# Splitting the token dimension of the first FFN's up-projection: two products of 256 tokens with the same weights in the place of one of 512

## The reference

```python
def swiglu_ffn(x, wi, wo):
    g, u = jnp.split(x @ wi, 2, axis=-1)      # wi: 1024 x 5632
    return (jax.nn.silu(g) * u) @ wo          # wo: 2816 x 1024

for i in range(DEPTH):                        # DEPTH = 2
    x = x + 0.5 * swiglu_ffn(rmsnorm(x, ffn1_norm[i]), ffn1_wi[i], ffn1_wo[i])
    ...                                       # mLSTM and window attention, merged
    x = x + 0.5 * swiglu_ffn(rmsnorm(x, ffn2_norm[i]), ffn2_wi[i], ffn2_wo[i])
    ...
```

## Time and profile before

| | |
|---|---|
| runs | 3436.26, 3437.9, 3438.53 us; median 3437.9 |
| the profiled execution | 3438.94 us, span 3437.2 us |
| PE busy | 3404.9 us (99%), 15506 products |
| PEld busy | 2747.4 us (80%), 15506 loads |
| DVE, ACT, POOL busy | 1599.5, 1040.8, 1546.8 us |
| mean granted clock of TensorE | 0.997 of 2.4 GHz |

### The profile page before, as it was taken

The page is one execution under the profiler, slowest core; times in us unless marked ns, Lnnn a source line. Parts: engine busy times, 40 slices in busy tenths (PEclk is TensorE's granted clock), DMA queues, the critical chain, the costliest instruction groups (busy, mean ns, idle before and its releaser), DMA issues.

```text
span 3437.2 us, 43454 instructions
## 1 busy us (share of the span) xinstructions
PE 3404.9 (99%) x15506; PEld 2747.4 (80%) x15506; DVE 1599.5 (47%) x1957; ACT 1040.8 (30%) x1383; POOL 1546.8 (45%) x1160
## 2 busy tenths in 40 slices
PE   8999999999999999999999999999999999999998
PEld 7888876788888888887678888877788887778887
DVE  5442235754423544223665442377480726647161
ACT  3222234332222322223433222246421123632112
POOL 4444432354444444443335444443354443335452
PEclk9999999999999999999999999999999999999999
DMA  4332322233333333342223333332233323223332
GB/s 149 98 97 94 110 74 68 74 98 98 98 103 93 93 96 98 98 111 74 62 74 104 98 93 103 95 93 48 68 98 98 98 92 81 51 65 108 94 98 80
DMA packets 496157, 311.25 MB, mean 91 GB/s; under 512 B 41792, under 2 KB 454827, under 8 KB 496043
## 3 DMA queue, kind: packets, MB, share of 16 engines
q1 hardware_dynamic: 494316, 307.21, 30.4%
q10 hardware_dynamic: 1727, 2.45, 0.2%
HBM read 305.94 MB, written 3.67 MB: 90 GB/s over the span
## 4 chain that ended last, share of the span: by engine, by line
issue 54%; POOL 35%; PE 10%; POOLq 1%; DVE 0%; DMA 0%; ACT 0%; ACTq 0%; DVEq 0%
POOL wl L488 35%; PE bank L507 2%; PE bank L511 2%; PE bank L512 2%; PE bank L530 1%; PE bank L526 1%; PE bank L532 1%; POOLq L485 0%; POOLq L483 0%; PE bank L533 0%; DMA onehot<-in_onehot_dram 0%; DVE x_sb L1748 0%; DVE acc L2340 0%; ACT out_tok L1668 0%; POOLq L488 0%
## 5 line engine op out<-in xcount | busy, mean ns | idle before, releaser
L488 POOL TENSOR_TENSOR wl<-raw,wh 128x512 fp32r<-128x512 f32 x1152 | 1545.7, 1364 | 1853.3 <-ACT wh L1288 1853.1
L1288 ACT ACTIVATE wh<-raw 128x1024 fp32r<-128x1024 f32 x576 | 608.2, 1057 | 1578.7 <-PE bank L507 747.0
L526 PE MATMUL bank<-xh,wh 128*128 128x512 f32 x2384 | 933.4, 392 | 0.0
L530 PE MATMUL bank<-xl,wh 128*128 128x512 f32 x2384 | 928.4, 389 | 0.0
L532 PE MATMUL bank<-xh,wl 128*128 128x512 f32 x2086 | 812.6, 390 | 0.0
L526 PEld LDWEIGHTS bank<-xh,wh 128*128 128x128 f32 x2384 | 448.0, 188 | 105.0 <-issue 12.3
L530 PEld LDWEIGHTS bank<-xl,wh 128*128 128x128 f32 x2384 | 448.2, 188 | 91.9
L507 PE MATMUL bank<-hh,wh 128*128 128x512 f32 (+1 forms) x1216 | 473.2, 389 | 0.0
L512 PE MATMUL bank<-hh,wl 128*128 128x512 f32 (+1 forms) x1216 | 473.0, 389 | 0.0
L511 PE MATMUL bank<-hl,wh 128*128 128x512 f32 (+1 forms) x1216 | 473.0, 389 | 0.0
L532 PEld LDWEIGHTS bank<-xh,wl 128*128 128x128 f32 x2086 | 392.0, 188 | 81.9
(11 more groups left out here) (390 smaller groups left out, 3112.9 us busy)
## 6 DMA issues: line engine op xcount, KB each, us to landing
raw<-in_ffn_wi_dram SPq DMA_DIRECT2D x176, 512.0 KB, 3.7
raw<-in_mlp_w_dram SPq DMA_DIRECT2D x128, 512.0 KB, 3.8
raw<-in_w_in_dram SPq DMA_DIRECT2D x102, 512.0 KB, 3.6
raw<-in_ffn_wo_dram SPq DMA_DIRECT2D x88, 512.0 KB, 3.6
raw<-in_w_out_dram SPq DMA_DIRECT2D x32, 512.0 KB, 3.8
raw<-in_w_ple_gate_dram SPq DMA_DIRECT2D x16, 512.0 KB, 3.8
raw<-in_w_a_dram SPq DMA_DIRECT2D x8, 512.0 KB, 3.4
raw<-in_w_b_dram SPq DMA_DIRECT2D x8, 512.0 KB, 3.3
```

What stands on the lines that cost most here:

```text
L488: last = gp.tensor_tensor(wl[j][:, part], raw[j % RAW_SLOTS][:, part], wh[j][:, part].bitcast(F32), ALU.subtract)
L526: first = pe.matmul(out[0:width, :], h[:, c:c + width], rh[:, k, :], start=k == 0, stop=False)
L530: pe.matmul(out[0:width, :], h[:, c:c + width], rl[:, k, :], start=False, stop=False)
L1288: act.activation(wh[n % SPLIT_SLOTS][:], raw[n % RAW_SLOTS][:], ACT.Copy).then_inc(s.hi_ready, 1)
```

## The change

In the ten-pass loop of each layer's first FFN (k = 0), each product of 512 tokens becomes two products of 256 tokens, first the left half of the bank and then the right half, with the same stationary tile. The order of the three kinds of product and of the eight feature tiles stays. The signal `slab_used` leaves with the unit's first half product, `tile_ready` with the last one. The second FFN's loop (k = 2), `first_units`, the down-projections and all other engines' programs stay as they are.

```diff
+            def unit_by_halves(B, L, n, t, rh, rl, i, step):
+
+                take_slab(B, L, n, i, step)
+                out = open_tile(B, L, t, i, step)
+                h, l = wh[n % SPLIT_SLOTS], wl[n % SPLIT_SLOTS]
+                for kt in range(KT):
+                    w = slice(kt * P, (kt + 1) * P)
+                    for a, b in ((h, rh), (h, rl), (l, rh)):
+                        for half in range(2):
+                            tok = slice(half * 2 * P, (half + 1) * 2 * P)
+                            last = pe.matmul(out[:, tok], a[:, w], b[:, kt, tok], start=kt == 0 and a is h and b is rh and half == 0,
+                                             stop=kt == KT - 1 and a is l and half == 1)
+                            if kt == 0 and a is h and b is rh and half == 0:
+                                last.then_inc(s.slab_used, 1)
+                last.then_inc(s.tile_ready, 1)
...
                 with pe.Fori(1, FT // 2) as i:
                     for u in range(4):
-                        unit(Block1, L, n + u, t + u, xh, xl, i, 4)
+                        if k == 0:
+                            unit_by_halves(Block1, L, n + u, t + u, xh, xl, i, 4)
+                        else:
+                            unit(Block1, L, n + u, t + u, xh, xl, i, 4)
```

## The result

The kernel after the change takes 3463.6 us (median of 6 runs, 3462.1 to 3464.3) where the one before takes 3438.9 us (6 runs, 3436.3 to 3442.0): a ratio of 1.0072, with a 95% interval of 1.0059 to 1.0084, some 24.7 us more. The prediction was 3440.5 us in a range of 3435 to 3466. The range holds the time, but only because it reached up to a rival's price; the forecast's own range (3435 to 3445) doesn't hold it, and "slower by over 0.2%", which had a chance of 0.37, came true. The profiled execution took 3464.2 us, its span 3462.4 us.

A forecast was written before the change was run, and what follows sets the result against it. TensorE, busy 3404.9 of 3437.2 us, was taken to bound the kernel. 3840 half products at 0.7 ns more each added 2.6 us to 3438.9, nothing for issue or clock: 3441.5, or 3440.5 for the median; range 3435 to 3466.

The forecast's parts named there:

- slower by over 0.2%: Whole kernel more than 6.9 us slower, summed from several rivals and half of the unforeseen; chance 0.37.
- What bounds the kernel: Whole kernel: TensorE, busy 3404.9 of 3437.2 us, sets the pace; what it spends more or less, the kernel does.
- (b): Edited loops: every half product has its own weight load; loads repeat at 111.7 ns, so they fit with little room.
- the column law: TensorE products: the loss goes by the moving column, 17/16, 0.4427 ns a column, so 113.3 ns for 256.
- (a): Edited loops: how long 256 columns occupy TensorE, 113.3 ns if loss goes by column, 120.1 if by instruction; column chosen.
- A rest that belongs to each product: Edited loops: possible fixed remainder per half product, taken as 0.7 ns, giving 114.0 ns and +2.6 us for 3840.
- (c): Edited loops: issuing and fetching twice as many instructions, 192 more a pass; costed at nothing.
- The rival with 3474 us: Jumps back at the edited loops' ends refetch instructions, 2 to 4 us for each of 18 jumps; chance 0.09.
- The clock: Edited loops: TensorE keeps full clock since it stays busy without a gap; nothing taken for it.
- A cost for each product: Edited loops: 13.4 ns lost per product whatever its columns, 120.1 ns a half product, kernel 3464 us; chance 0.14.
- the middle value: Edited loops: loads and stream now and then wait for each other, 115.1 to 118 ns, kernel 3450 us; chance 0.12.
- two readers of memory, now both active nearly all the time, slow each other: Edited loops: stated way to be wrong, load and stream slowing each other, distance above 115 ns without gaps.

The follow-up runs named there:

- Experiment 7: Changed kernel's edited loop, each unit waiting until earlier tiles were taken out, units cut as 512, 256+256, 384+128 and 320+192 columns: 3598.8 us.
- experiment 3: Edited loop with weight tiles of 128, 96, 64, 32 columns: 256+256 took 120.0, 116.0, 113.3, 113.3 ns a product; 512 took 226.8, 229.9, 229.8, 231.7.
- experiment 4: Edited loop's operands read as other types: 256 columns took 113.3 ns (bf16, 4 bytes apart), 109.2 (bf16 neighbours), 119.9 (kernel's type); bf16 512 4 bytes apart, 225.0.
- experiment 2: Changed kernel with weight tiles of 64 columns instead of 128, half of the result left out: 3435.8 us, 113.3 ns a product instead of 120.0.
- experiment 5: Edited loop's operands read from other addresses: 256 columns took 116.7 ns (moving shifted by 8), 113.3 (weights shifted by 16), 111.7 (one moving column repeated); in place 120.0.

## Why the prediction was right or wrong

**What bounds the kernel** was right. All of the 25.6 us came from the distance of products on TensorE, and nothing else in the page moved; no wait, clock or transfer has a part in it.

**(b), the second load**, was right in its facts: 3840 loads for 3840 products, a floor of 111.7 ns, met again with 111.7 by four times 128 columns and by one moving column. What was wrong is the sentence drawn from them, "The loads fit, with little room". They fit in time and yet aren't free. A load alone takes some 108 ns (the prediction's reading of the first product after a wait), so by estimate a load was at work for about half of each 226.7 ns and is now for nine tenths of each 120.0; beside these addresses that costs 6.7 ns a product. The Trainium skill ("TensorE: Matmul & The Clock Gate", Step-by-step) says of a running matmul that loading the next tile's weights "doesn't steal SBUF read bandwidth" from it. The runs agree for the uncut product in place (226.7 ns, the column law) and for the cut one with weights shifted by 16 columns (113.3), and not for the changed kernel; where they differ, the measured 120.0 against 113.3 ns decides.

**(a), the column or the instruction.** The choice was between two laws for one number, 13.4 ns, and the column was the right one: bf16 words 4 bytes apart show it, and loads of 64 columns bring the cut product to 113.3 ns. The step that failed is the next, "A rest that belongs to each product can't be excluded ... so I add half of that, 0.7 ns, and take 114.0 ns". The rest measured 6.7 ns, nearly ten times the 0.7: 3840 x 6.67 = 25.6 us instead of 2.6. (Half of the 2 ns of that sentence would have been 1.0 and not 0.7, 3.8 us; that slip decides nothing.) The rest isn't a constant of a product, so a line through the earlier trace rows could not find it. Both points of that line are first products behind a pause. Experiment 7 gives for 256 columns the same law in that place (222 ns) and 0.12 us from then on. The 36 columns of the earlier trace rows misled in the same manner. I read them as 0.23 us "again", and so "the loss isn't the load's reading beside the stream". With two decimals the rows couldn't show what the means of the same trace do:

```profile
L507 PE MATMUL mb<-xh,gate_h 128*36 128x512 f32 x16 | 6.3, 393 | 0.0
```

393 ns where a full load has 389, so some 230 ns from start to start and not 226.7. These weights are narrower and lie elsewhere; which of the two counts isn't shown, but that a smaller load can go with a slower uncut product, as in experiment 3, stood in the trace before, and with it that load and stream may not be independent. What is true in the sentence is that the 13.4 ns of 512 columns aren't the load's. The prediction also says that "no row has 256 columns". There are some in straight code, at 216 ns, but as plain float32, whose products take twice the time of the kernel's type (experiment 4's units of plain float32: 215.8 ns for 256 columns, 429.1 for 512), so they would not have helped.

**(c), issue and fetching**, was right: 83 packets, two more, and no gap behind the fourth unit of a pass. The queue moved nothing from 60 us to the end of the first loop or from 1190 us to the end of the second, so none of the 18 jumps back fetched anything. The rival with 3474 us is out.

**The clock** stayed at 1.00 in both windows, as forecast.

**The rivals.** "A cost for each product" had the time to within a microsecond (3464 against 3463.6) and the windows exactly (230.6 forecast, 230.4 measured), but experiments 2, 3 and 5 refute the mechanism; that 13.4 / 2 and the 6.7 ns of the loads agree is, as far as the runs show, chance. The right mechanism stood in the middle value ("loads and stream, both near their limit, now and then wait for each other"), which I gave 115.1 to 118 ns and 0.12, and in the last sentence, "two readers of memory, now both active nearly all the time, slow each other". Both had its place and sign; its size was put too low, and it isn't "now and then": 1916 of 1920 distances in the loop are 120 ns. Together the middle value and the cost for each product had 0.26, and the range reached far enough because the price of the second was in it. That it holds the time is luck: the mechanism that carried it up there isn't at work.

**What stays open.** Which property of the addresses decides. The shift of the weights by 16 columns takes the cost from the cut product and puts it on the uncut one; I have one such shift, one of the moving tile (by 8 columns, half of the cost gone), one stride that changes nothing, and no map. Why the first products behind a pause escape the cost isn't shown either. The cut product with shifted weights kept 113.3 ns in each of its ten units, but a whole loop of such units wasn't tried, and for pairs only two distances between the places were (256 and 128 columns).

## What to carry to other kernels

- Where the weight load lasts nearly as long as the stream beside it, cutting a product isn't neutral even if both fit: price a cut from rows in which loads and products of that size follow each other without a pause, never from the first product behind a wait.
- When a forecast hits a number, try its mechanism too; here one run with half the weights' width parted them.
- Before cutting or reordering products, try the order in which one product reads its columns: two places in turn gave 4.2% of this kernel.

## What the runs showed of the hardware

- Reading a moving operand of 4-byte steps in order at full clock costs 1/16 (226.7 ns for 512 columns, 225.0 for bf16 words 4 bytes apart); from two places 256 columns apart it is 215.8, from one column over and over 215.8, from four places 283.3, from sixteen 434.5, with every second column first 451.7.
- Beside loads of 128 stationary columns a product took between 0 and 7 ns more than the column law, by addresses and sizes: 0 for 512 columns, 3.4 to 5.1 for 272 to 480, 6.7 for 256; 16 columns' shift of the weights turns it round (113.3 and 233.2 ns). Narrower loads don't always take less: beside 32 stationary columns 512 moving ones took 231.7 ns.
- With a load for each, products of the kernel's type followed each other no faster than 111.7 ns on average with 128 columns of weights, and 60 ns with 64. Bf16 neighbours, 128 columns of weights and 128 moving ones, did so in 55.8.
- Plain 32-bit floats took 215.8 ns for 256 columns and 429.1 for 512, two clocks a column and little above.
